# A two-block transformer kernel: one small table grown by 32 bytes and two 32-byte pads, which move most of SBUF by 32 bytes

## The reference

```python
def reference(...):
    x = first_block(...)     # layer 0: mLSTM + short conv mixer, layer 1: grouped attention
    return second_block(...) # two layers: pooling + spatial gating mixer, gated MLP with a conv
# in each layer of the first block
x = x + mod_x[2] * mixer(rms_norm(x) * (1 + mod_x[1]) + mod_x[0])
x = x + mod_x[5] * (square(relu(h @ w1)) @ w2)        # w1: 1024 x 4096, w2: 4096 x 1024
# in each layer of the second block
x = layernorm(ALPHA * x + gate1 * (concat(pool(a), sgu(u, v)) @ w_out))
f = (gelu(causal_dwconv(h @ w_up_gate)) * (h @ w_up_value)) @ w_down   # 1024 x 2 x 2816, 2816 x 1024
x = layernorm(ALPHA * x + gate2 * f)
```

## The kernel before

| operand | stage | start before | modulo 64 |
|---|---|---|---|
| `Whi`, `Wlo` | weights, all stages | 57472, 41088 | 0 |
| `h0_hi`, `h0_lo` | input of layer 0's mixer | 178112, 202688 | 0 |
| `mixa_*`, `mixb_*` | mixer output of layer 0 (6 of 8 blocks) | 178112 and on | 0 |
| `mixc_hi`, `mixc_lo` | mixer output of layer 0 (2 of 8 blocks) | 118688, 124832 | 32 |
| `h1_*`, `h2_*`, `h3_*`, `hid0_*`, `hid1_*` | first block's MLPs and attention input | from 118688 | 32 |
| `ao_*` | attention output | 118688, 135072 | 32 |
| `hs_*`, `ms_*`, `hid2_*` | second block | from 118688 | 32 |
| `AK`, `AQ`, `AV` | attention's keys, queries, values (float32, one pass) | from 167840 | 32 |
| `PT` | turned probabilities, streamed (float32) | 200960 | 0 |

## Time and profile before

### The profile page before, as it was taken

How to read it: one execution, slowest core, us unless ns; L and a number is a source line. 1 busy time by engine, 2 the same in 40 slices (tenths; PEclk the granted TensorE clock), 3 DMA queues, 4 the chain that set the end, 5 groups by cost and what they waited for, 6 DMA issues and landing times.

```text
span 2627.3 us, 36055 instructions
## 1 busy us (share of the span) xinstructions
PE 2563.2 (98%) x13872; PEld 2124.3 (81%) x13872; DVE 1632.6 (62%) x2569; ACT 964.2 (37%) x1425; POOL 95.9 (4%) x185
## 2 busy tenths in 40 slices
PE   7999999999999999999999999999999999999998
PEld 4888888888888886669888887888888788888886
DVE  6777556654546556656555566675656876644446
ACT  4333533131313245764332243353232454532224
POOL 0000000000000000000000000000000000000000
PEclk9999999999999999999999999999999999999999
DMA  6432213433333321002544553234445422222222
GB/s 260 139 107 95 99 60 128 161 113 112 112 104 129 103 67 47 1 9 95 179 152 161 174 176 108 83 119 153 156 155 193 144 101 81 81 93 92 96 96 88
DMA packets 82937, 303.66 MB, mean 116 GB/s; under 512 B 9200, under 2 KB 11376, under 8 KB 81520
## 3 DMA queue, kind: packets, MB, share of 16 engines
q1 hardware_dynamic: 56736, 206.82, 23.1%
q0 software_dynamic: 26064, 94.91, 10.7%
HBM read 299.60 MB, written 2.10 MB: 115 GB/s over the span
## 4 chain that ended last, share of the span: by engine, by line
PE 93%; DVE 4%; ACT 1%; issue 1%; DMA 1%; SPq 0%; DVEq 0%; ACTq 0%
PE G L494 20%; PE G L496 20%; PE G L495 20%; PE G L521 5%; PE G L522 5%; PE G L523 5%; PE B L1024 2%; PE G L580 1%; PE G L582 1%; PE G L581 1%; PE G L986 1%; PE B L1000 1%; DVE Wlo L1712 1%; PE G L667 1%; PE G L669 1%
## 5 line engine op out<-in xcount | busy, mean ns | idle before, releaser
L1140 ACT ACTIVATE Whi<-Wraw 128x1024 fp32r<-128x1024 f32 x357 | 374.9, 1051 | 463.6 <-DMA Wraw<-wstream_dram 456.4
L1712 DVE TENSOR_TENSOR Wlo<-Wraw,Whi 128x1024 fp32r<-128x1024 f32 x357 | 436.4, 1222 | 128.0 <-ACT Whi L1140 126.8
L494 PE MATMUL G<-h_hi,Whi 128*128 128x512 f32 (+1 forms) x1024 | 361.0, 353 | 0.3 <-ACT T L1239 0.3
L496 PE MATMUL G<-h_hi,Wlo 128*128 128x512 f32 (+1 forms) x1024 | 358.7, 350 | 0.0
L495 PE MATMUL G<-h_lo,Whi 128*128 128x512 f32 (+1 forms) x1024 | 358.3, 350 | 0.0
L494 PE MATMUL G<-hs_hi,Whi 128*128 128x512 f32 x720 | 287.3, 399 | 4.1 <-DVE Wlo L1712 4.1
L496 PE MATMUL G<-hs_hi,Wlo 128*128 128x512 f32 x720 | 284.4, 395 | 0.0
L495 PE MATMUL G<-hs_lo,Whi 128*128 128x512 f32 x720 | 284.4, 395 | 0.0
L496 PE MATMUL G<-hid_hi,Wlo 128*128 128x512 f32 (+1 forms) x760 | 280.0, 368 | 0.0
L494 PE MATMUL G<-hid_hi,Whi 128*128 128x512 f32 (+1 forms) x760 | 279.9, 368 | 0.0
L495 PE MATMUL G<-hid_lo,Whi 128*128 128x512 f32 (+1 forms) x760 | 279.7, 368 | 0.0
(11 more groups left out here) (484 smaller groups left out, 4588.5 us busy)
## 6 DMA issues: line engine op xcount, KB each, us to landing
Wraw<-wstream_dram SPq DMA_DIRECT2D x357, 512.0 KB, 3.3
Araw<-adaw_dram POOLq DMA_DIRECT2D x180, 512.0 KB, 4.1
FIRST<-firstw_dram SPq DMA_DIRECT2D x6, 1024.0 KB, 21.8
X<-xin_dram SPq DMA_DIRECT2D x4, 1536.0 KB, 11.2
out_dram<-X SPq DMA_DIRECT2D x16, 128.0 KB, 1.7
ROW<-rows_dram SPq DMA_DIRECT2D x2, 768.0 KB, 7.6
CB<-cvec_dram SPq DMA_DIRECT2D x2, 512.0 KB, 10.8
CB<-cvec_dram POOLq DMA_DIRECT2D x1, 512.0 KB, 4.8
```

The source lines that it names most:

```text
L494: pe.matmul(o, wh, hi[:, a:b], start=(k == 0), stop=False)
L496: last = pe.matmul(o, wl, hi[:, a:b], start=False, stop=(k == kt - 1))
L1140: act.activation(Whi[:, t % 4, :], Wraw[:, t % 4, :], ACT.Copy).then_inc(w_hi, 1)
L1712: dve.tensor_tensor(Wlo[:, t % 4, :], Wraw[:, t % 4, :], Whi[:, t % 4, :].bitcast(F32), ALU.subtract).then_inc(w_lo, 1)
```

## The change

The table `small` is made 64 numbers wide, 256 bytes instead of 224; its uses, up to column 56, stay as they are. All that follows it in the stack begins 32 bytes later, at 118720. Behind `HV` and behind `KR` an unused tensor of 32 bytes is put in, so that what follows these two doesn't fall back to 32 modulo 64; it starts 64 bytes later than before.

```diff
+        def line(name, where=ctx):
+
+            where.enter_context(nc.sbuf_tensor(f"{name}_line", [P, 8], F32))
...
-        small = sb("small", [P, 56])
+        small = sb("small", [P, 64])
         RCOL = small[:, 32:56]
...
         HV = sb("HV", [P, TT, MH, DV + 1], where=hyb)
+        line("HV", hyb)
         CY = sb("CY", [P, 4, 772], where=hyb)
...
         KR = sb("KR", [P, 2, 2 * TT], where=att)
+        line("KR", att)
         ROPE = sb("ROPE", [P, 2, NX], where=att)
```

## The result

The changed kernel takes **2604.81 us** (median of four runs, 2603.45 to 2614.23), the kernel before 2631.55 us beside it (2627.86 to 2633.46). The ratio is 0.9906 with a 95% interval of 0.9891 to 0.9922: faster by 26.7 us, where 29.7 were forecast.

A forecast was written before the change was run, and what follows sets the result against it. TensorE was taken to bound the kernel; 6912 matmuls of 512 columns at 4.3 ns less each save 29.7 us, with nothing counted for other moves. So 2632.99 - 29.7 = 2603.3 us, range 2598 to 2610 us (8 in 10).

The forecast's parts named there:

- The bound: Whole kernel: TensorE sets the time, busy for 2563.2 of 2627.3 us and holding 93% of the chain.
- the rival with a lost gain: Waits for weights or VectorE replace part of the gain; 2618 us at half gain; chance 0.06 beyond the range.
- The term of 4.3 ns: Saving per 512-column three-pass matmul moved from 32 to 0 modulo 64: 6912 matmuls, 29.7 us.
- The third sign: Mean matmul durations of two groups, 395.0 ns for `hid` and 391.8 for `h0`: a difference of 3.2 ns.
- the comparison inside one product: Layer 0's mixer output, 512 columns: `mixc` at 233.3 ns against 228.6 for `mixa` and `mixb`, 4.7 ns.
- 0 or 32 modulo 64: Claim that streams starting at 0 modulo 64 are cheap and those at 32 cost 4.3 ns more per 512-column matmul.
- just where `h0`, `mixa` and `mixb` stand before: Claim that the moved bulk goes to 64 modulo 128, the start of the rows already cheap before.
- The smallest term: `h0` going from 64 to 0 modulo 128 in the first 300 us: counted as nothing.
- The bound of 2.6 us: Limit on `h0`'s gain or loss: 4.3 ns on 600 matmuls, 2.6 us either way.
- The start doesn't matter: Rival: any multiple of 32 bytes costs the same; time stays at 2633 us, give or take 2.6; chance 0.04.
- Its explanation by the region of SBUF: That rival's reason for the 4 ns: `mixc` lies low in SBUF, `mixa`, `mixb` and `h0` high; within its 0.04.
- Everything on one beat: Rival: streams and weights starting alike modulo 64 collide; 2662.7 us at 4.3 ns lost on 6912 matmuls; chance 0.02.

The follow-up runs named there:

- the profiled execution: The one of the changed kernel's first four runs that was profiled, the slowest of them: 2614.23 us, with a span of 2612.6 us.
- the first repeat: Profile from running the unmodified changed kernel again, four runs: median 2604.05 us, ratio 0.9892 to the kernel before.
- experiment 3: Changed kernel with `small` at 80 numbers, all operands behind it 64 bytes further, the weights not: 2634.32 us, ratio 1.0005 to the kernel before.
- experiment 6: Changed kernel with `small` at 96 numbers, all operands behind it 128 bytes further: 2627.89 us, ratio 0.9996 to the kernel before.
- experiment 7: Kernel before with the weights moved from 128 to 96 modulo 256, every stream kept in place modulo 256: 2611.72 us, ratio 0.9922.
- The second repeat: Profile from running the unmodified changed kernel a third time, two runs: median 2606.74 us, ratio 0.9905 to the kernel before.
- experiment 8: Changed kernel with `small` at 112 numbers, the bulk starting where the weights do modulo 256: 2598.43 us, ratio 0.9875 to the kernel before.
- experiment 4: Small kernel without the computation, sweeping stream and weight starts and pauses: 226.7 to 234.3 ns per 512-column matmul.
- experiment 9: Small kernel without the computation, weights at 128 modulo 256, stream start swept in 4- and 16-byte steps: 226.7 to 240.0 ns for 512 columns.

## Why the prediction was right, and where it was wrong

**The bound.** Right. TensorE holds 93% of the chain before and after, and its busy time fell by as much as the span: 15.2 and 14.7 us in the profiled execution, 28.1 and 26.9 in the first repeat, where some 29 were forecast. No wait took the place of the time removed, so the rival with a lost gain had no place; VectorE at 68% in the tightest stage kept its cover.

**The term of 4.3 ns.** Right in size. Leaving out `h0` and `mix`, the 6864 matmuls of the other four stages took 1607.0 us before and 1578.1 in the first repeat: 28.9 us, 4.2 ns each. The third sign, 3.2 ns between the durations of two groups, was the weaker one as said: `hid`'s own durations fell by 4.6 ns (395.0 to 390.4), its distances by 4.4. One bound doesn't follow from its terms: 3.2 ns alone give 22.1 us and thus 2610.9, and with something given back more, where the range ends at 2610.

**What the 4.3 ns belong to.** Wrong. The prediction took the comparison inside one product and read it as "0 or 32 modulo 64". The trace of before held two distances only, 32 for the bulk and 64 for `h0`, `mixa` and `mixb`, and both readings fit them equally; experiments 3, 6 and 7 part them. It came out right since the change brings the bulk to distance 64, the very distance of the cheap rows. The prediction's sentence that the bulk would stand "just where `h0`, `mixa` and `mixb` stand before" was true, and carried the sum whichever modulus counts. The rule as such was a guess among several that these rows allowed; with it alone, the places of experiments 3 and 6 would have been forecast as fast too.

**The smallest term.** Here the step failed. "I take nothing, as the two starts are alike in the modulo that the rows show to count": the rows did not show it to count. `h0` and most of `mix` went from distance 64 to 128. In the first repeat the 512 columns of the two stages took 2.2 and 0.4 us more (table), and the 256 columns of `h0`, for which nothing was counted, went from 116.9 to 118.9 ns, 1.2 us over 600. The bound of 2.6 us, kept for the range, held the 512-column part; taking it as a loss gives 2605.9 us. The layer 0 mixer got 3.3 us longer in the first repeat, which 2.2 + 1.2 account for.

**The rest of the gap** between the profiles. In the profiled execution the mixer got 5.9 us longer, not 3.3. The windows of the kernel after, at 49.0 and 103.6 us (busy time of PE, PEld, DVE, ACT, POOL, then the granted clock, the DMA share and GB/s), followed by the same two of the repeat:

```profile
49.00:52.40 3.40, 3.40 (x13) 2.87 (x13) 3.00 (x6) 1.12 (x2) 0.00 (x0) 0.54 0.00 0
103.60:107.00 3.40, 3.40 (x18) 3.40 (x19) 0.33 (x1) 3.01 (x5) 0.00 (x0) 0.54 0.76 231
```

```profile
49.00:52.40 3.40, 3.26 (x20) 2.88 (x20) 2.52 (x6) 1.16 (x3) 0.00 (x0) 1.00 0.00 0
103.60:107.00 3.40, 3.40 (x28) 3.26 (x27) 0.52 (x1) 2.82 (x5) 0.00 (x0) 1.00 0.58 208
```

TensorE ran nearly all of these two stretches at 1.2 GHz in one execution (13 and 18 matmuls in 3.4 us) and at 2.4 GHz in the other (20 and 28). Two times 3.4 us at half speed would lose 3.4 us in sum (an estimate from these rows); 2.6 show. The second repeat has both stretches and a mixer of 261.8 us as well. The MLP of layer 0 is 6.6 us shorter in the first repeat than in the other two, with the same time for 512 columns: there the 256 columns ran at 113.6 instead of 117.7 ns, the other of the two rhythms. And the second block lost 812.2 - 805.9 = 6.3 us to the slow stretch at its end. These three, 15.5 us in sum, set the profiled execution behind the first repeat; their spans differ by 12.2 us, and the 3.3 us that go the other way were not assigned. That they also make the range of the runs without a profile, some 5 to 10 us, which hides a term of 2 us, is likely and not shown.

**The rivals.** "The start doesn't matter" would have given 2633 us and falls with experiment 3, where the same kernel 64 bytes on takes 2634. Its explanation by the region of SBUF falls as well: `h0` turned slow and the bulk fast in their old regions. "Everything on one beat" predicted a loss if streams and weights start at the same point; experiment 8 puts them there modulo 256 and it is the fastest place for 512 columns. For 256 columns that rival has a small truth in it, 120.0 against 117.5 ns. That the weights' start has to do with it was thus in the prediction, with the wrong sign.

**Why the distance counts** is argued, not shown. In the trace most weight loads start 2 to 4 ns after a matmul's start and run beside it, so it may be that both read SBUF at once at a fixed lag, and that the distance sets which part each is in. The page "TensorE: Matmul & The Clock Gate" of the Trainium skill, section "Step-by-step: what each phase is for", says TensorE has two independent read ports, so that a load takes nothing from the stream. By that rule I would expect the weights' address not to matter; experiments 4 and 7 disagree, by 226.7 to 233.3 ns for the same stream. **Still open:** what starts the slow rhythm of 512 columns at distance 64. It was seen in one of three profiles, from 2246 us on, behind a wait that the others have too, and no pause in experiment 4 brought it back. Experiment 9 shows two rhythms for 256 columns and at a few other distances of 512; that this is the same thing is likely and not shown.

## What to carry to other kernels

Where TensorE loads new weights for every matmul and sets the time, work out the stream's start less the weights' start modulo 256, with both at multiples of 32 bytes, and put the costliest group at 0 or 64 if it is of 512 columns (for 256 columns 0 was among the dear ones, 120.0 ns); then read it off the distances between starts in the timeline, not the durations. When two groups of rows differ in speed, write down everything in which they differ before naming one modulus: here the operands that "already stood right" were the ones that lost. A small kernel that sweeps one address in a few hundred microseconds would have shown the rule before the change was costed.

## What the runs showed of the hardware

- A three-pass (`fp32r`) matmul of 512 columns with a weight load each costs 226.7 to 240.0 ns from start to start at 2.4 GHz, depending on the two addresses and, at some of them, on what ran before (experiments 4 and 9); of 256 columns 113.3 to 123.3 ns. The best distance isn't the same for both widths.
- The same instructions at the same addresses can hold either of two rhythms for hundreds of microseconds: 228.9 or 233.3 ns for 512 columns (from 2246 us to the end, one profile), 113.6 or 117.7 ns for 256 on average (a whole MLP, one profile against two).
- TensorE's granted clock fell to 1.2 GHz in stretches of 3.4 to 13.7 us, most of them at the stages' edges, and once more at the end; 59.2 us in sum before and 66.8, 66.6 and 66.5 us in the three profiles of the kernel after. These three have eight stretches each, but not at the same places: two fall into layer 0's mixer in the first and the third, none does in the second. Each costs up to half its length, an estimate from the two clocks; the two in the mixer, 3.4 us each, cost 2.6 us in sum.
